# Score matmuls of the gated recurrence, in one group per head or one block at a time between the projection's matmuls

## What is computed

```python
bc = jnp.cumsum(to_chunks(log_f, HG_F), axis=3)
b_ref = bc[:, :, :, HG_CHUNK // 2 - 1:HG_CHUNK // 2, :]
scores = jnp.einsum('bhntf,bhnsf->bhnts', qc * jnp.exp(bc - b_ref), kc * jnp.exp(b_ref - bc))
scores = jnp.where(causal, scores, 0.0)
o_intra = jnp.einsum('bhnts,bhnsv->bhntv', scores, vc)
...
state = dec_n[..., None] * state + jnp.einsum('bhsf,bhsv->bhfv', k_n, v_n)
```

## Time and profile before

| what | value |
|---|---|
| median of 3 runs | 837.37 us (837.19 to 838.29) |
| the profiled execution | 837.19 us, its span 835.4 us |
| TensorE busy | 819.5 us, 98% of the span |
| VectorE busy | 503.1 us, 60% |
| ScalarE busy | 348.7 us, 42% |
| chain that ended last | 94% on TensorE |
| DMA | 87.52 MB, mean 105 GB/s |

### The profile page before, as it was taken

How to read it: one execution, slowest core, us unless ns; L and a number is a source line. 1 busy time by engine, 2 the same in 40 slices (tenths; PEclk the granted TensorE clock), 3 DMA queues, 4 the chain that set the end, 5 groups by cost and what they waited for, 6 DMA issues and landing times.

```text
span 835.4 us, 10178 instructions
## 1 busy us (share of the span) xinstructions
PE 819.5 (98%) x4111; PEld 696.8 (83%) x4111; DVE 503.1 (60%) x556; ACT 348.7 (42%) x393; POOL 20.8 (2%) x30
## 2 busy tenths in 40 slices
PE   7999999999999999999999999999999999999994
PEld 7989988899888888888888889888888888888883
DVE  3647645567364424414428685885669566957698
ACT  4549343494335223232225025653545345435430
POOL 1100100000001000000000010000000000000000
PEclk9999999999999999999999999999999999999998
DMA  9541313313113323323723407017301810270002
GB/s 311 194 151 52 101 51 101 101 50 100 51 58 97 111 89 100 100 100 100 301 100 93 159 4 250 1 51 252 101 0 51 302 51 0 81 272 1 0 1 100
DMA packets 68215, 87.52 MB, mean 105 GB/s; under 512 B 1581, under 2 KB 51798, under 8 KB 68182
## 3 DMA queue, kind: packets, MB, share of 16 engines
q1 hardware_dynamic: 68182, 87.06, 31.0%
HBM read 84.96 MB, written 2.10 MB: 104 GB/s over the span
## 4 chain that ended last, share of the span: by engine, by line
PE 94%; DVE 4%; issue 1%; DMA 1%; DVEq 0%; SPq 0%; ACT 0%
PE bank L1267 30%; PE bank L1268 30%; PE bank L1269 30%; DVE two L1167 1%; PE bank L1437 1%; DVE two L1179 1%; DMA two<-in_mem_dram 1%; PE bank L1479 0%; PE bank L1431 0%; PE bank L1402 0%; PE bank L1547 0%; PE bank L1294 0%; DVE two L1184 0%; DVE w_lo L760 0%; DVE decay L1173 0%
## 5 line engine op out<-in xcount | busy, mean ns | idle before, releaser
L1267 PE MATMUL bank<-x_hi,w_hi 128*128 128x512 f32 (+1 forms) x704 | 268.5, 381 | 0.0
L1269 PE MATMUL bank<-x_hi,w_lo 128*128 128x512 f32 (+1 forms) x704 | 267.2, 380 | 0.0
L1268 PE MATMUL bank<-x_lo,w_hi 128*128 128x512 f32 (+1 forms) x704 | 267.2, 380 | 0.0
L755 DVE TENSOR_TENSOR w_lo<-raw,w_hi 128x2048 fp32r<-128x2048 f32 x40 | 91.4, 2290 | 107.7 <-ACT w_hi L473 107.4
L1269 PEld LDWEIGHTS bank<-x_hi,w_lo 128*128 128x128 f32 x704 | 132.4, 188 | 25.1
L1267 PEld LDWEIGHTS bank<-x_hi,w_hi 128*128 128x128 f32 x704 | 132.4, 188 | 24.7
L1268 PEld LDWEIGHTS bank<-x_lo,w_hi 128*128 128x128 f32 x704 | 132.5, 188 | 24.4
L1267 PE MATMUL bank<-w_hi,y_hi 128*128 128x512 f32 (+1 forms) x320 | 121.5, 380 | 0.4 <-DVE two L1167 0.4
L1269 PE MATMUL bank<-w_hi,y_lo 128*128 128x512 f32 (+1 forms) x320 | 121.1, 379 | 0.0
L1268 PE MATMUL bank<-w_lo,y_hi 128*128 128x512 f32 (+1 forms) x320 | 121.1, 378 | 0.0
L473 ACT ACTIVATE w_hi<-raw 128x2048 fp32r<-128x2048 f32 x40 | 76.4, 1915 | 41.5 <-PE bank L1269 36.8
(11 more groups left out here) (180 smaller groups left out, 834.6 us busy)
## 6 DMA issues: line engine op xcount, KB each, us to landing
raw<-in_w_in_dram SPq DMA_DIRECT2D x28, 1024.0 KB, 5.0
raw<-in_w_up_dram SPq DMA_DIRECT2D x16, 1024.0 KB, 8.8
small<-in_w_down_dram SPq DMA_DIRECT2D x12, 1024.0 KB, 7.0
raw<-in_w_branch_dram SPq DMA_DIRECT2D x6, 1024.0 KB, 5.0
raw<-in_w_o_dram SPq DMA_DIRECT2D x4, 1024.0 KB, 5.1
raw<-in_w_down_dram SPq DMA_DIRECT2D x4, 1024.0 KB, 4.7
two<-in_x_dram SPq DMA_DIRECT2D x2, 1024.0 KB, 11.4
small<-in_w_mem_v_dram SPq DMA_DIRECT2D x2, 1024.0 KB, 12.0
```

Source lines behind the costliest of these rows:

```text
L755: dve.tensor_tensor(w_lo[:, slot, :], raw[:, r, :], w_hi[:, slot, :].bitcast(F32), ALU.subtract)\
L1267: pe.matmul(dst, a[0], b[0], start=first, stop=False, skip_group_check=goes_on)
L1268: pe.matmul(dst, a[0], b[1], start=False, stop=False, skip_group_check=goes_on)
L1269: return pe.matmul(dst, a[1], b[0], start=False, stop=last, skip_group_check=goes_on)
```

## The change

The function `scores(h)`, which issues the 16 matmuls of a head in one piece (four 128-column matmuls, then q = 3 for all blocks, q = 2, q = 1), becomes `score_block(h, b)`, which issues the four matmuls of one block (128 columns, then q = 1, 2, 3). Instead of all 16 behind k = 4 of tile 9 (head 0) and tile 10 (head 1), one block goes behind each of k = 1, 3, 5 and 7. The wait for the eighth operand and for the bank stands behind k = 1; the semaphore that tells of the head's scores comes with the last matmul behind k = 7, which is behind the tile's own last matmul. Operands, results and the number of matmuls are the same.

```diff
-                def scores(h):
+                def score_block(h, b):
...
-                    for b in range(TB):
-                        mm = pe.matmul(t[:, blk(b)], aa[:, h, blk(b)], ee[:, h, blk(b)], start=True, stop=True)
-                    for q in (3, 2, 1):
-                        for b in range(TB):
-                            now = slice(b * P + q * C, b * P + (q + 1) * C)
-                            n = h * TB + b
-                            keys = (lf[:, h, b * P:b * P + C], k_two[:, n, :], k_three[:, n, :])[q - 1]
-                            mm = pe.matmul(t[0:q * C, now], keys, qq[:, h, now], start=True, stop=True)
+                    n = h * TB + b
+                    pe.matmul(t[:, blk(b)], aa[:, h, blk(b)], ee[:, h, blk(b)], start=True, stop=True)
+                    for q in range(1, QD):
+                        now = slice(b * P + q * C, b * P + (q + 1) * C)
+                        keys = (lf[:, h, b * P:b * P + C], k_two[:, n, :], k_three[:, n, :])[q - 1]
+                        mm = pe.matmul(t[0:q * C, now], keys, qq[:, h, now], start=True, stop=True)
                     return mm
...
-                        if k != 4:
+                        if k % 2 == 0:
                             return
-                        if h == 0:
-                            pe.wait_ge(operands, half * OPERANDS + 8)
-                        begin_aux(HALF, "sc%d" % h, half)
-                        scores(h).then_inc(aux_done, 1)
+                        if k == 1:
+                            if h == 0:
+                                pe.wait_ge(operands, half * OPERANDS + 8)
+                            begin_aux(HALF, "sc%d" % h, half)
+                        mm = score_block(h, k // 2)
+                        if k == KD - 1:
+                            mm.then_inc(aux_done, 1)
```

## The result

The changed kernel takes 842.41 us (median of 6 runs, 840.45 to 842.79) against 837.83 us for the kernel before in the same comparison: a ratio of 1.0052, 95% interval 1.0042 to 1.0062. In a second comparison, on another occasion, it took 842.79 against 836.92 us: 1.0069, 1.0057 to 1.0081. So it is slower by 0.5 to 0.7%; 842.6 us had been predicted.

A forecast was written before the change was run, and what follows sets the result against it. TensorE, busy 98% of the span, was taken as the bound. Sixteen blocks at 1.00 us against 10.7 us now add 5.3 us: 842.5 from the profiled 837.19, 842.7 from the median, stated as 842.6, range 841.3 to 844.6.

The forecast's parts named there:

- What bounds the kernel: TensorE, busy 98% of the span: what its stream gains or loses reaches the end nearly one for one.
- The block's sum: One score block between projection matmuls, added from trace starts: 1.455 us, less 0.45 for two projection steps, 1.00 us.
- the drain behind the 128-column record: Within a block, the 32-column weight load waits behind the second 128-column record: 0.275 less 0.07, 0.20 us.
- the step into 96 columns: Within a block, from the first 96-column record to the second: 0.11 us, estimated from the 32- and 64-column steps.
- The total: All 16 score blocks on TensorE: 16.0 us against 10.7 for the four groups now, +5.3 us.
- The cross-check: Second sum for TensorE's added time: 36 more width switches at 0.115, 4.1 us, plus 12 more exits, 1.2 us.
- Early entry and later end: Waits moved to k = 1 and scores complete behind k = 7: both covered by margins, priced at nothing.
- The margin at the transposes: From the end of L928 on the vector engine to TensorE's transposes: shrinks from 2.46 to about 0.26 us.
- Rival A: Leaving a block, 96 to 128 columns drains too: 1.8 us on top, 844.5 us; chance 7%.
- B: Vector chain ends late and TensorE stands at the transposes twice: 843.1 to 844.1 us; chance 8%.
- C: Width switches in separate blocks cost nothing behind wide matmuls: +0.7 us, 838.1, no measurable change; chance 6%.
- D: Wide stream hides weight loads and switches, only moving columns count: 6.4 us instead of 10.7, 833.1; chance 3%.

The follow-up runs named there:

- The runs with 96 columns: Changed kernel and kernel before, each with 96-column keys for all quarter matmuls; judged by trace, loop's stream 210.2 and 209.8 us.
- desc: Changed kernel with the widths falling in each block (128, 96, 64, 32); 841.89 us against 836.82 for the kernel before, ratio 1.0061.
- moved: Kernel before, groups of 16 kept whole, head 0's behind k = 1 and head 1's behind k = 7; 836.92 against 836.82 us, ratio 1.0001.
- k3: Changed kernel with the transposes of lf behind k = 3 of tile 11 instead of k = 4; judged by trace, loop's stream 214.8 against 214.2 us.
- s96: Changed kernel with 96-column keys and 96 output rows for all three quarter matmuls; judged by trace, loop's stream 210.2 us against 208.6 before.

## Why the prediction held, step by step

- *What bounds the kernel.* Right. TensorE's waits in the changed kernel are again four, 1.5 us the longest, none at the scores or the transposes, and the 5.6 us added to its stream reach the end (588.2 us behind it in both).
- *The block's sum.* 1.455 us predicted, 1.46 measured, with its terms: the drain behind the 128-column record (0.20) had been carried over from other predecessors, and the step into 96 columns (0.11) extrapolated; both were right to 0.01.
- *The total.* 5.3 us predicted, 5.6 measured in the stream. The term left out: the four projection steps from 99.28 to 100.21 take 0.93 us instead of 4 x 0.227 = 0.91, and this hangs on each piece. 12 more pieces are 0.2 us. The rest is rounding of the block.
- *The cross-check* failed in its parts, though its sum was near. It gave 36 switches 0.115 each, 4.1 us, and 12 exits 0.1 each, 1.2 us. The runs with 96 columns give the 12 more pieces 0.4 us in all, 0.03 each. The 4.1 us for the switches are near what they cost in the order they were read in (`desc`, 4.7 - 0.4 = 4.3); the change's own order makes it 5.2, which a single price for all switches can't tell. That two errors, 0.8 too much and 1.1 too little, nearly cancel is luck; the block's sum, which has the order in it, needed none.
- *Early entry and later end.* Priced at nothing, and `moved` shows nothing. The margin at the transposes was put at 0.26 us; it is 0.28 by the records and 0.38 by what it takes to lose time (`k3`).
- *Rival A* (a drain on the way out of 96 columns) falls: the projection's load starts at 98.94, while the last 96-column record is under way. *B* falls, no wait on L928 in the change. *C* and *D*, no drain or all hidden behind the wide matmuls, fall with 1.46 us a block.
- *The time.* 842.6 against 842.41 and, in the second comparison, 842.79. The agreement to 0.2 us is closer than the method: the kernel before itself came out at 837.37, 837.83 and 836.92, so the difference was 4.6 us in one comparison and 5.9 in the other, and the 5.6 of the stream lies between. The range's low end does not follow from its own working: 842.6 - 1.1 is 841.5, not 841.3.

## What to carry to other kernels

Small matmuls put in between wide ones are not free filler: each one whose weights have another column width class than its neighbours' (128 and 96 here, 64, 32) stops TensorE until the matmul before it is nearly out, 0.12 to 0.15 us a time in this kernel, and the wide matmul behind it hides none of it. (A narrow matmul straight behind a 512-column one was not tried: every block starts with 128 columns.) So sort narrow matmuls by width and keep them together, even over heads and tiles, as far as the buffers and the hand-offs allow; if they must be spread, use one width class for all and take the longer loads. When the bottleneck engine runs without waits, add up starts from the trace, one small piece at a time, and check that every consumer of the moved result still has its margin. When two kernels differ by less than their front does by chance, compare the stretch between two instructions that stand in both.

## What the runs showed of the hardware that was not expected

- 96-column weights behave as 128-column ones: no gap in either direction (128 to 96 in the earlier trace rows, 96 to 128 at 98.94 above, and no gap at all in `s96`). "TensorEngine Tiling (Array Packing)" of the Trainium skill, Tiling Modes, lists column tilings of 128, 64 and 32 only, which fits: 96 columns is a case of 128.
- A weight load that came 0.44 us late behind a 512-column matmul cost 0.3 us (`k3`): some 0.15 us of it was absorbed.
- The front of this kernel, up to L1349, is what makes its runs differ. In the 12 profiles it takes 36.7 to 39.4 us, without relation to the edit, while the loop's stream of the changed kernel came out at 214.2 and 214.1. The first 20 us of before, of the changed kernel and of its repetition:

```profile
0.00:20.00 20.00, 15.59 (x105) 15.09 (x106) 7.61 (x10) 8.39 (x12) 3.42 (x17) 0.91 0.93 308
```

```profile
0.00:20.00 20.00, 16.49 (x123) 15.52 (x124) 7.52 (x10) 8.54 (x12) 3.41 (x17) 1.00 0.91 304
```

```profile
0.00:20.00 20.00, 16.51 (x110) 15.54 (x111) 7.52 (x10) 8.66 (x12) 3.43 (x17) 1.00 0.92 306
```

  The wait for the first memory tokens was 2.2 us before and 1.3 in the changed kernel, and the mean granted clock of this stretch 0.91 and 1.00. The repetition has the same wait and the same mean as the changed kernel and still takes 1.3 us more to L1349. The column doesn't show it, but the steps of the first projection matmuls do. The kernel before, from a stretch with a granted clock of 0.50:

```profile
9.50:10.50 1.00, 1.00 (x7) 1.00 (x6) 0.05 (x1) 0.00 (x0) 0.00 (x0) 0.50 1.11 350
...
9.52 0.41 PE L1268 MATMUL bank<-y_lo,w_hi 128*128 128x256 f32 x1
9.73 0.41 PE L1269 MATMUL bank<-y_hi,w_lo 128*128 128x256 f32 x1
```

  The changed kernel, and then its repetition:

```profile
7.66 0.36 PE L1267 MATMUL bank<-y_hi,w_hi 128*128 128x256 f32 x1
7.86 0.28 PE L1268 MATMUL bank<-y_lo,w_hi 128*128 128x256 f32 x1
7.97 0.28 PE L1269 MATMUL bank<-y_hi,w_lo 128*128 128x256 f32 x1
```

```profile
8.82 0.56 PE L1267 MATMUL bank<-y_hi,w_hi 128*128 128x256 f32 x1
9.18 0.41 PE L1268 MATMUL bank<-y_lo,w_hi 128*128 128x256 f32 x1
9.40 0.41 PE L1269 MATMUL bank<-y_hi,w_lo 128*128 128x256 f32 x1
...
9.77 0.28 PE L1268 MATMUL bank<-y_lo,w_hi 128*128 128x256 f32 x1
9.89 0.28 PE L1269 MATMUL bank<-y_hi,w_lo 128*128 128x256 f32 x1
```

  A step between two such matmuls takes 0.21 us in the kernel before at the lower level of TensorE's clock (9.52 to 9.73), and 0.12 in the changed kernel (7.86 to 7.97). The repetition starts at the slow pace (9.18 to 9.40) and has the fast one from 9.77 on; by its first projection matmul it is 1.16 us behind (8.82 against 7.66), which is most of the 1.3. So what differs is mainly how long TensorE works at the lower level of its clock. A comparison of two single profiles by their spans would have put the change at 3.8 us instead of 5.6.
